# State-space part: the exchange of real and imaginary halves as SBUF to SBUF transfers instead of fp32 products on TensorE

## The chip, the cores and the metric

The kernel runs on one core of a Trainium2 chip. The metric is the device time of one execution, in microseconds (us).

## What the reference computes

One layer of a hybrid model for 1024 new tokens of one stream (`TP`) and 64 further tokens of a running one (`TS`), 1088 in all (`T`): an RMS norm, one large input projection, three branches (a pooling mixer, a state-space mixer, an attention with forget gates), three sigmoid gates per channel that weigh the branches, an output projection, and a gated feed-forward layer with a short convolution. The change is in the state-space mixer:

```python
lam_bar = jnp.exp(lam * dt)                        # complex, per state
bu = jnp.einsum('gpc,blgc->blgp', b_bar, ug)       # 32 groups, 64 complex states, 16 channels each
_, states = lax.associative_scan(combine, (a, bu), axis=1)   # s[t] = lam_bar * s[t-1] + bu[t]
y = jnp.einsum('gcp,blgp->blgc', c_mat, states).real.reshape(bn, L, W_MIX)
```

## The kernel before

There are two stages, and the state-space mixer stands at the start of the second (`mix_engines`). Each engine has its own list of instructions, executed in order, and engines meet at semaphores. `Steps` counts a semaphore through named steps, so `pe_did.at("v1")` means "TensorE has done step v of tile 1".

The state-space mixer works on four tiles (`t` = 0 to 3) of 8 groups (`NB`) each. Time is cut into chunks of 16 tokens (`C`), 68 of them (`NCH`). The 64 complex states lie on the 128 partitions, real parts on partitions 0 to 63 and imaginary parts on 64 to 127. For each tile:

- TensorE transposes the input matrices (step `et`, L2009), makes the kernel of the chunk (step `k`, L2015) and the inputs of the chunks (step `v`, L2024). ScalarE copies the last from PSUM to `vv` (L2129), 8 groups by 70 columns (`E70`), so 560 fp32 per partition.
- SyncE's list (`toeplitz`, L1889) spreads the chunk kernel in 16 SBUF to SBUF transfers over `tm1` and `tm0`, 8 KB for the smallest and 128 KB for the largest. It does so as soon as step `k` has been copied out.
- The recurrence over chunks has a complex factor, whose angle is taken out first so that VectorE's scan (L2254) is real: `vv` is multiplied by the cosine table (`rc`, L2245) and its copy with exchanged halves by the sine table (`rs`, L2249), and the two are subtracted. After the scan the result `ww` is turned back in the same way (L2256, L2260) and gives `sc` (L2265, L2266), the states ahead of each chunk.
- The copy with exchanged halves is made on TensorE: a product with a 128 by 128 permutation `swap` in fp32, two products of 280 columns each, for `vv` (step `swap_v`, L2030) and for `ww` (step `swap_w`, L2035). The results are read from PSUM.
- TensorE makes the output of the chunks (step `y`, L2042 to L2044) from the input, `tm1`, `tm0` and `sc`, and turns it back (step `back`, L2056).

So that TensorE has work while the others do this, 39 pieces of the gate projection stand between these steps (`gate_pieces`, 24 matmuls each through the helper line L154, or `three_pass`). `SLOTS` says how many follow each step: between `v` and `y` there are three pieces in tiles 0 and 3 and four in tiles 1 and 2. GpSimd splits the gate weights into a high and a low part for these pieces (`split_tile`, L951 to L955), and SyncE's list loads them (`load_gate`): blocks 15 and 16 after the `toeplitz` of tile 0, 19 and 20 after that of tile 1, 23 after that of tile 2, none after that of tile 3. Each such load waits until GpSimd has split the block that held the buffer. VectorE scales each piece (L2183) and ScalarE finishes and stores it.

Of the kernel before, what the change touches and what calls it, by code (L numbers as in the profile page):

```python
# [14 lines left out]
ALU, ACT, AX = mybir.AluOpType, mybir.ActivationFunctionType, mybir.AxisListType  # L15

P = 128
# [18 lines left out]
G32, SC, SS = 32, 16, 64  # L36
NB = 8
E70 = NP_CH + 1 + NS_CH + 1
# [6 lines left out]
class Steps:  # L45
# [15 lines left out]
    def mark(self, name):  # L61
        assert self.names[self.n % len(self.names)] == name, (self.names[self.n % len(self.names)], name)
        self.n += 1
        return self.sem, 1
# [1681 lines left out]
SEVEN = ("et", "k", "v", "swap_v", "swap_w", "y", "back")  # L1746
# [25 lines left out]
def mix_engines(nc, m, io, sems):  # L1772

    ps, sem = m.bank, lambda n: sems(f"mix_{n}")
    gp, r4 = ps[:, 0:4], ps[:, 4:8]
    CS, KP0 = C * SC, 96
    GATE0, NG = GATES_ATT, 3 * (3 * KD - GATES_ATT)
    flat = lambda t: t[:].rearrange("p g e -> p (g e)")
    with ExitStack() as outer:
        y = outer.enter_context(nc.sbuf_tensor("y", [P, MW, T], F32))  # L1780
        with ExitStack() as inner:
            sb = lambda n, s, d=F32: inner.enter_context(nc.sbuf_tensor(n, s, d))
            et, swap = sb("et", [P, 2 * NB, P + 8]), sb("swap", [P, P])
            assert nc.sbuf_base == m.early_at
            sb("early", [P, EARLY // 4])
            m.tab.append(sb("tab1", [P, NB, NTAB]))
            rows = sb("ssm_rows", [P, NB * CS])
            u2 = sb("u2", [P, 2, 2 * NB, NCH])
            cl = sb("cl", [P, NB, C + 1, SC])
            tm1, tm0 = sb("toeplitz1", [P, NB, CS]), sb("toeplitz0", [P, NB, CS // 2])  # L1790
            vv, x1, x2, d0 = (sb(n, [P, NB, E70]) for n in ("vv", "x1", "x2", "d0"))
            sc, sf = sb("sc", [P, NB, NCH]), sb("sf", [P, G32, 2])
            gout = sb("gate_out3", [P, T])
        with ExitStack() as inner:
            sb = lambda n, s, d=F32: inner.enter_context(nc.sbuf_tensor(n, s, d))
            merged, prod, gate = sb("merged", [P, KD * T]), sb("prod", [P, T]), sb("gate", [P, 2, T])
            sig = sb("sig", [P, 2, T])
            yh, yl = sb("y_hi", [P, MW, T], F32R), sb("y_lo", [P, MW, T], F32R)
    ww = x2
# [7 lines left out]
    tiles = range(MW)  # L1807
# [7 lines left out]
    b2_ld, even_mm, prod_done, sum_done, hi, lo = (sem(n) for n in (  # L1815
        "b2_ld", "even_mm", "prod_done", "sum_done", "hi", "lo"))
    ws, gws = m.merge_ws, m.gate_ws
    pe_did = Steps(sem("pe_did"), [f"{n}{t}" for t in tiles for n in SEVEN])
    act_did = Steps(sem("act_did"), [f"{n}{t}" for t in tiles for n in (
        ("et", "kp", "s0_", "vv") + (tuple(f"gelu_hi{k}_" for k in range(3)) if t == 3 else ()) + ("yc",))] +  # L1820
        ["gelu_hi3_3"] + [f"sig{o}" for o in tiles] + [f"r_hi{o}" for o in tiles])
# [8 lines left out]
    halves = lambda t: t[:].rearrange("p g e -> p (g e)").rearrange("p (b n) -> p b n", b=2)  # L1830
# [17 lines left out]
    def sync(sp):  # L1848
        def load_tab(t):
            if t >= 2:  # L1850
                sp.wait_ge(*pe_did.at(f"y{t - 2}"))
            sp.dma_start(tab[t % 2][:], m.tab_d[:, t * NB:(t + 1) * NB]).then_inc(tab_ld[t % 2], 16)
# [28 lines left out]
        def toeplitz(t):  # L1881
# [4 lines left out]
            for r in range(C):  # L1886
                rows = slice(r % 8 * SC, (r % 8 + 1) * SC)
                dst, c0, cn = (tm1, (C - 1 - r) * SC, CS) if r >= 8 else (tm0, (7 - r) * SC, CS // 2)
                sp.dma_start(dst[rows, :, c0:cn], kp[:, :, 0:cn - c0]).then_inc(tm_ld, 16)  # L1889

        load_tab(1)
        load_frames(0)
        for t in tiles:
            load_u(t)
        for t, (early, late) in enumerate((((14,), (15, 16)), ((17, 18), (19, 20)), ((21, 22), (23,)), ((), ()))):
            for n in early:
                load_gate(n)
            if t == 3:
                load_glu(0)
                load_glu(1)  # L1900
            toeplitz(t)
            for n in late:
                load_gate(n)
            if t < 3:
                load_frames(t + 1)
            if t < 2:
                load_tab(t + 2)
# [68 lines left out]
    def tensor(pe):  # L1976
# [21 lines left out]
            return mm  # L1998

        gate_pieces(0, "start")  # L2000
        pe.wait_ge(consts, 2)
        for t in tiles:
            j = t % 2
            if t:
                pe.wait_ge(*dve_did.at(f"yt{t - 1}"))
            pe.wait_ge(*pool_did.at(f"w{t}"))
            for n in range(2 * NB):
                g, h = n // 2, n % 2
                mm = pe.transpose(r4[:, n // 4, n % 4 * P:(n % 4 + 1) * P], w[:, g, 8 * h:8 * h + 8], m.ident[:])  # L2009
            mm.then_inc(*pe_did.mark(f"et{t}"))  # L2010
            gate_pieces(t, "et")
            pe.wait_ge(*act_did.at(f"et{t}"))
            pe.wait_ge(*dve_did.at(f"et{t}"))
            for g in range(NB):
                mm = pe.matmul(r4[0:SC, g // 2, g % 2 * CS:(g % 2 + 1) * CS], tab[j][:, g, B1:B1 + SC],  # L2015
                               cl[:, g, 0:C], start=True, stop=True)
            mm.then_inc(*pe_did.mark(f"k{t}"))
            gate_pieces(t, "k")
            pe.wait_ge(*act_did.at(f"kp{t}"))
            pe.wait_ge(*dve_did.at(f"kp{t}"))  # L2020
            pe.wait_ge(u2_ld[j], 256 * (t // 2 + 1))
            for g in range(NB):
                for h in range(2):
                    mm = pe.matmul(r4[:, g // 4, g % 4 * NCH:(g % 4 + 1) * NCH], et[:, 2 * g + h, 0:P],  # L2024
                                   u2[:, j, 2 * g + h], start=h == 0, stop=h == 1)
            mm.then_inc(*pe_did.mark(f"v{t}"))
            gate_pieces(t, "v")
            pe.wait_ge(*act_did.at(f"vv{t}"))
            for h in range(2):
                mm = pe.matmul(r4[:, h, 0:NSW], swap[:], halves(vv)[:, h], start=True, stop=True)  # L2030
            mm.then_inc(*pe_did.mark(f"swap_v{t}"))
            gate_pieces(t, "swap_v")
            pe.wait_ge(*dve_did.at(f"ww{t}"))
            for h in range(2):
                mm = pe.matmul(r4[:, h, 0:NSW], swap[:], halves(ww)[:, h], start=True, stop=True)  # L2035
            mm.then_inc(*pe_did.mark(f"swap_w{t}"))
            gate_pieces(t, "swap_w")
            pe.wait_ge(*dve_did.at(f"sc{t}"))
            pe.wait_ge(tm_ld, 256 * (t + 1))
            for g in range(NB):  # L2040
                out = r4[0:NCH, g // 2, g % 2 * CS:(g % 2 + 1) * CS]
                pe.matmul(out, u2[:, j, 2 * g + 1], tm1[:, g], start=True, stop=False)  # L2042
                pe.matmul(out[:, CS // 2:CS], u2[:, j, 2 * g], tm0[:, g], start=False, stop=False)
                mm = pe.matmul(out, sc[:, g], cl[:, g, 1:C + 1], start=False, stop=True)  # L2044
            mm.then_inc(*pe_did.mark(f"y{t}"))
            gate_pieces(t, "y")
            if t == MW - 1:
                pe.wait_ge(ws.w_split, 3)
                pe.wait_ge(gate_raw, NG)
                for k in range(3):  # L2050
                    pe.wait_ge(*dve_did.at(f"y_lo{k}_3"))
                    part(0, 0, operand["glu"], [k])
            pe.wait_ge(*act_did.at(f"yc{t}"))
            pe.wait_ge(*dve_did.at(f"yc{t}"))
            for n in range(C):
                mm = pe.transpose(r4[:, n // 4, n % 4 * NCH:(n % 4 + 1) * NCH], yc[:, n], m.ident[0:NCH, 0:NCH])  # L2056
            mm.then_inc(*pe_did.mark(f"back{t}"))
            gate_pieces(t, "back")
# [31 lines left out]
    def scalar(act):  # L2090
# [20 lines left out]
        for t in tiles:  # L2111
# [20 lines left out]
            gate_pieces(t, "swap_v")  # L2132
            gate_pieces(t, "swap_w")
            if t == MW - 1:
                act.wait_ge(*pe_did.at(f"swap_w{t}"))
                act.wait_ge(piece_mm, NG)
                for k in range(3):
                    gelu_high(k)
# [38 lines left out]
    def vector(dve):  # L2177
# [19 lines left out]
        dve.wait_ge(m.o_st[2], 32 + 32 * HEADS)  # L2197
        for g in range(3):
            dve.wait_ge(m.g_st[g], 16 * GATES_ATT)
        for a in range(2):  # L2200
            dve.tensor_copy(swap[:, a * SS:(a + 1) * SS], m.ident[:, (1 - a) * SS:(2 - a) * SS])
        dve.memset(tm1[:], 0.0)
        dve.memset(tm0[:], 0.0)
        dve.memset(vv[:, :, 0:1], 0.0)
# [4 lines left out]
        for t in tiles:  # L2209
# [30 lines left out]
            gate_pieces(t, "k")  # L2240

            rc, rs = tab[j][:, :, RC:RC + E70], tab[j][:, :, RS:RS + E70]
            sw = lambda b: r4[:, b, 0:NSW].rearrange("p (g e) -> p g e", e=E70)
            dve.wait_ge(*act_did.at(f"vv{t}"))
            dve.tensor_tensor(x1[:], vv[:], rc, ALU.mult).then_inc(*mark("x1"))  # L2245
            gate_pieces(t, "v")
            dve.wait_ge(*pe_did.at(f"swap_v{t}"))
            for b in range(2):
                ins = dve.tensor_tensor(x2[:, 4 * b:4 * b + 4], sw(b), rs[:, 4 * b:4 * b + 4], ALU.mult)  # L2249
            ins.then_inc(*mark("x2"))  # L2250
            dve.wait_ge(*at("x2"))
            dve.tensor_tensor(x1[:], x1[:], x2[:], ALU.subtract).then_inc(*mark("d1"))
            dve.wait_ge(*at("d1"))
# [1 line left out]
            dve.wait_ge(*at("ww"))  # L2255
            dve.tensor_tensor(x1[:], ww[:], rc, ALU.mult).then_inc(*mark("x3"))  # L2256
            gate_pieces(t, "swap_v")
            dve.wait_ge(*pe_did.at(f"swap_w{t}"))
            for b in range(2):
                ins = dve.tensor_tensor(vv[:, 4 * b:4 * b + 4], sw(b), rs[:, 4 * b:4 * b + 4], ALU.mult)  # L2260
            ins.then_inc(*mark("x4"))
            dve.wait_ge(*at("x4"))
            dve.tensor_tensor(sf[:, t * NB:(t + 1) * NB], x1[:, :, NP_CH:E70:NS_CH + 1],
                              vv[:, :, NP_CH:E70:NS_CH + 1], ALU.add).then_inc(*mark("sf"))
# [749 lines left out]
```

## Time and profile before

| | |
|---|---|
| median of 3 runs | 1903.46 us (1899.62 to 1903.72) |
| the profiled execution | 1899.79 us, of it the span of the profile 1898.0 us |
| TensorE busy | 98% of the span |
| VectorE, GpSimd, ScalarE busy | 63%, 43%, 23% |
| granted TensorE clock, mean | 0.993 of full speed |
| SyncE's DMA queue | 31.6% of 16 engines' span |

Engines are PE (TensorE), PEld (its weight loads, which overlap), DVE (VectorE), ACT (ScalarE), POOL (GpSimd) and SP (SyncE). An engine's name with a q means its instruction queue, where DMAs are issued. L154 is line 154 of the kernel. Idle time is put down to the engine or DMA that released the waiting instruction last. Matmuls overlap, so that a row's duration is longer than the distance to the next row. The four tiles of the state-space mixer lie between about 594 and 825 us of the span.

### The profile page before, as it was taken

Reading aid. Unit: us, or ns where it says so; the run is one execution under the profiler, and the core shown is the slowest. Engines: PE = TensorE matmul, PEld = TensorE weight load, DVE = VectorE, ACT = ScalarE, POOL = GpSimd, SP = SyncE. Lnnn points to the kernel's source line nnn. Section 1 sums busy time; section 2 is a strip of 40 time slices with the busy share of each in tenths; the row PEclk is TensorE's granted clock in tenths of the full one; section 3 lists DMA queues with packets and bytes.
Section 4 is the critical chain, followed back from the end, with each engine's and each line's share of the span. In section 5 each row is a group of like instructions: output and inputs, shape, how many; then the busy total and the mean of one; then the engine's idle time right before and its main releaser. Section 6 shows DMA issues by size and latency. Waiting matters only on the chain. (4 is left out here: it accounts for less than half of the span.)

```text
span 1898.0 us, 28823 instructions
## 1 busy us (share of the span) xinstructions
PE 1854.0 (98%) x11323; PEld 1804.3 (95%) x11323; DVE 1193.7 (63%) x1820; ACT 433.0 (23%) x812; POOL 807.0 (43%) x461
## 2 busy tenths in 40 slices
PE   7999999999999999999999999999999999999997
PEld 6989999999989898999999999999999999999997
DVE  6788653888875545542673667557557557557556
ACT  4210123556641111140010231111111111111113
POOL 4434444333356446322232454625625625625520
PEclk8999999999999999999999999999999999999999
DMA  8634829676625454356441111101101101101102
GB/s 271 186 126 129 264 106 261 159 189 172 173 83 144 116 118 100 68 219 229 137 163 45 35 54 56 56 22 55 55 22 55 55 22 55 52 26 55 45 23 97
DMA packets 221950, 203.97 MB, mean 107 GB/s; under 512 B 58306, under 2 KB 200622, under 8 KB 221155
## 3 DMA queue, kind: packets, MB, share of 16 engines
q1 hardware_dynamic: 205650, 170.46, 31.6%
q10 hardware_dynamic: 16208, 32.25, 4.8%
q8 instruction: 62, 1.02, 0.2%
q14 instruction: 30, 0.24, 0.0%
HBM read 138.44 MB, written 59.77 MB: 104 GB/s over the span
## 5 line engine op out<-in xcount | busy, mean ns | idle before, releaser
L154 PE MATMUL bank<-act_hi,w_hi 128*128 128x364 f32 (+1 forms) x2544 | 849.1, 334 | 8.5 <-DVE act_lo L1483 3.7
L154 PE MATMUL bank<-act_lo,w_hi 128*128 128x364 f32 (+1 forms) x2544 | 839.1, 330 | 0.0
L154 PE MATMUL bank<-act_hi,w_lo 128*128 128x364 f32 (+1 forms) x2544 | 838.6, 330 | 0.0
L154 PEld LDWEIGHTS bank<-act_hi,w_hi 128*128 128x128 f32 x2544 | 480.5, 189 | 15.2 <-issue 9.2
L154 PEld LDWEIGHTS bank<-act_lo,w_hi 128*128 128x128 f32 x2544 | 480.3, 189 | 0.8
L154 PEld LDWEIGHTS bank<-act_hi,w_lo 128*128 128x128 f32 x2544 | 480.0, 189 | 0.0
L2769 DVE SCALAR_TENSOR_TENSOR conv<-up_raw,cw,conv 128x1090 f32<-128x1090 f32 x86 | 179.9, 2092 | 63.8 <-ACT up_raw L2655 33.5
L2452 POOL CAST w_hi<-w_raw 128x1024 fp32r<-128x1024 f32 x44 | 47.5, 1079 | 356.9 <-PE bank L154 351.8
L154 PE MATMUL bank<-ffn_hi,down_hi 128*128 128x364 f32 (+1 forms) x528 | 174.0, 330 | 0.7 <-DVE up_raw L2803 0.5
L154 PE MATMUL bank<-ffn_lo,down_hi 128*128 128x364 f32 (+1 forms) x528 | 173.0, 328 | 0.0
L154 PE MATMUL bank<-ffn_hi,down_lo 128*128 128x364 f32 (+1 forms) x528 | 172.7, 327 | 0.0
L2792 DVE TENSOR_TENSOR xt<-bank,xt 128x364 f32<-128x364 f32 (+1 forms) x240 | 113.4, 527 | 76.9 <-PE bank L154 76.3
L2761 DVE TENSOR_TENSOR up_raw<-bank,n_inv 128x364 f32<-128x364 f32 x129 | 58.0, 505 | 139.8 <-PE bank L154 139.6
L953 POOL CAST w_hi<-w_raw 128x1024 fp32r<-128x1024 f32 x36 | 46.0, 1278 | 201.2 <-PE bank L154 200.3
L2443 POOL TENSOR_TENSOR w_raw<-w_raw,vec 128x1024 f32<-128x1024 f32 x44 | 116.0, 2635 | 17.1 <-PE bank L154 13.0
L2454 POOL TENSOR_TENSOR w_lo<-w_raw,w_hi 128x1024 fp32r<-128x1024 f32 x44 | 109.4, 2487 | 3.5
L154 PEld LDWEIGHTS bank<-ffn_hi,down_hi 128*128 128x128 f32 x528 | 99.1, 188 | 1.4 <-DVE up_raw L2803 0.8
L154 PEld LDWEIGHTS bank<-ffn_lo,down_hi 128*128 128x128 f32 x528 | 99.4, 188 | 0.0
L154 PEld LDWEIGHTS bank<-ffn_hi,down_lo 128*128 128x128 f32 x528 | 99.0, 188 | 0.0
L2660 ACT ACTIVATE last<-up_raw 128x2 f32 (+1 forms) x86 | 13.4, 204 | 360.3 <-DVE up_raw L2762 355.5
L955 POOL TENSOR_TENSOR w_lo<-w_raw,w_hi 128x1024 fp32r<-128x1024 f32 x36 | 92.9, 2580 | 2.9
L1225 POOL CAST w_hi<-w_raw 128x1024 fp32r<-128x1024 f32 x20 | 24.7, 1236 | 147.8 <-PE bank L154 147.7
(302 smaller groups left out, 2462.6 us busy)
## 6 DMA issues: line engine op xcount, KB each, us to landing
w_raw<-in_w_up SPq DMA_DIRECT2D x44, 512.0 KB, 3.8
w_raw<-in_w_in SPq DMA_DIRECT2D x42, 512.0 KB, 4.8
gate<-gate_scratch ACTq DMA_DIRECT2D x24, 544.0 KB, 3.8
w_raw<-in_w_down SPq DMA_DIRECT2D x22, 512.0 KB, 3.3
gate_scratch<-gate_out ACTq DMA_DIRECT2D x48, 182.0 KB, 2.7
w_raw<-in_w_branch SPq DMA_DIRECT2D x12, 512.0 KB, 3.9
kh<-kh_scratch SPq DMA_DIRECT2D x16, 336.0 KB, 7.4
kl<-kl_scratch SPq DMA_DIRECT2D x16, 336.0 KB, 8.2
```

The costliest lines, as they stand in the source:

```text
L154: mm = pe.matmul(out, w(k), x(k)[:, c0:c0 + cn], start=first and k == ks[0] and n == 0, stop=last and k == ks[-1] and n == 2)
L953: pool.tensor_copy(m.wh[:, a], m.raw[:, a]).then_inc(s.w_hi, 1)
L955: pool.tensor_tensor(m.wl[:, a], m.raw[:, a], m.wh[:, a].bitcast(F32), ALU.subtract).then_inc(s.w_split, 1)
L1225: pool.tensor_copy(m.wh[:, a], m.raw[:, a]).then_inc(w_hi, 1)
L2443: pool.tensor_tensor(m.raw[:, a], m.raw[:, a], by_channel(m.vec[:, 8:16]), ALU.mult).then_inc(*pool_did.mark(f"sc_{blk}"))
L2452: pool.tensor_copy(hi[:, a], m.raw[:, a]).then_inc(*pool_did.mark(f"hi_{blk}"))
L2454: pool.tensor_tensor(lo[:, a], m.raw[:, a], hi[:, a].bitcast(F32), ALU.subtract).then_inc(*pool_did.mark(f"lo_{blk}"))
L2660: ins = act.activation(by_tile(last[:, n], 2)[:, bass.ds(f, 1)], up[:, a, c0:c0 + 2].unsqueeze(1), ACT.Copy)
L2761: dve.tensor_tensor(up[:, a, HP + c0:HP + c0 + n], acc[a][:, g, 0:n], inv[:, c0:c0 + n], ALU.mult)
L2769: dve.scalar_tensor_tensor(out=cv[:, a], in0=up[:, a, t:UP - 2 + t], scalar=m.cw01[:, bass.ds(f + 44 * t, 1)], in1=cv[:, a], op0=ALU.mult, ...
L2792: ins = dve.tensor_tensor(m.xt[:, d, c0:c0 + cn], acc[d % 2][:, g, 0:cn], m.xt[:, d, c0:c0 + cn], ALU.add)
```

## The change

The permutation `swap` and the 16 fp32 products are taken out, with their steps in `pe_did`. SyncE's list gets a function `exchange`, which copies partitions 0 to 63 of `vv` or `ww` to partitions 64 to 127 of a buffer and the other half the other way, in two transfers of 64 rows of 2,240 bytes. The two buffers (`other`) lie in the memory of `et`, which is free between step `v` and the next tile. In SyncE's list the first exchange stands behind `toeplitz(t)` and waits for `vv`; then come one gate load, a wait for `ww`, the second exchange, and the remaining loads. VectorE waits for the landing, and its products with the sine table read SBUF instead of PSUM, in one instruction of 560 columns instead of two of 280. The slots of the gate pieces stay as they were.

```diff
-            et, swap = sb("et", [P, 2 * NB, P + 8]), sb("swap", [P, P])
+            et, _ = sb("et", [P, 2 * NB, P + 8]), sb("gap", [P, P])
...
+    swapped = sem("swapped")
+    other = [flat(et)[:, n * NB * E70:(n + 1) * NB * E70] for n in range(2)]
...
+        def exchange(n, src):
+            for a in range(2):
+                sp.dma_start(other[n][SS * a:SS * (a + 1)], flat(src)[SS * (1 - a):SS * (2 - a)]).then_inc(swapped, 16)
...
             toeplitz(t)
-            for n in late:
+            sp.wait_ge(*pe_did.at(f"v{t}"))
+            sp.wait_ge(*act_did.at(f"vv{t}"))
+            exchange(0, vv)
+            for n in late[:1]:
+                load_gate(n)
+            sp.wait_ge(*dve_did.at(f"ww{t}"))
+            exchange(1, ww)
+            for n in late[1:]:
                 load_gate(n)
...
         gate_pieces(0, "start")
-        pe.wait_ge(consts, 2)
...
             gate_pieces(t, "v")
-            pe.wait_ge(*act_did.at(f"vv{t}"))
-            for h in range(2):
-                mm = pe.matmul(r4[:, h, 0:NSW], swap[:], halves(vv)[:, h], start=True, stop=True)
-            mm.then_inc(*pe_did.mark(f"swap_v{t}"))
             gate_pieces(t, "swap_v")
-            pe.wait_ge(*dve_did.at(f"ww{t}"))
-            for h in range(2):
-                mm = pe.matmul(r4[:, h, 0:NSW], swap[:], halves(ww)[:, h], start=True, stop=True)
-            mm.then_inc(*pe_did.mark(f"swap_w{t}"))
             gate_pieces(t, "swap_w")
             pe.wait_ge(*dve_did.at(f"sc{t}"))
...
             if t == MW - 1:
-                act.wait_ge(*pe_did.at(f"swap_w{t}"))
                 act.wait_ge(piece_mm, NG)
...
-        for a in range(2):
-            dve.tensor_copy(swap[:, a * SS:(a + 1) * SS], m.ident[:, (1 - a) * SS:(2 - a) * SS])
...
-            dve.wait_ge(*pe_did.at(f"swap_v{t}"))
-            for b in range(2):
-                ins = dve.tensor_tensor(x2[:, 4 * b:4 * b + 4], sw(b), rs[:, 4 * b:4 * b + 4], ALU.mult)
-            ins.then_inc(*mark("x2"))
+            dve.wait_ge(swapped, 64 * t + 32)
+            dve.tensor_tensor(x2[:], sw(0), rs, ALU.mult).then_inc(*mark("x2"))
...
-            dve.wait_ge(*pe_did.at(f"swap_w{t}"))
-            for b in range(2):
-                ins = dve.tensor_tensor(vv[:, 4 * b:4 * b + 4], sw(b), rs[:, 4 * b:4 * b + 4], ALU.mult)
-            ins.then_inc(*mark("x4"))
+            dve.wait_ge(swapped, 64 * t + 64)
+            dve.tensor_tensor(vv[:], sw(1), rs, ALU.mult).then_inc(*mark("x4"))
```

## Rows read from the trace of the kernel before

**Rows 1.** The page: busy time of each engine, share of the span, instructions.

```profile
PE 1854.0 (98%) x11323; PEld 1804.3 (95%) x11323; DVE 1193.7 (63%) x1820; ACT 433.0 (23%) x812; POOL 807.0 (43%) x461
```

**Rows 2.** Windows over the four tiles: busy time by engine, then clock, DMA.

```profile
595.00:660.00 65.00, 63.22 (x394) 57.02 (x393) 35.18 (x36) 10.12 (x20) 36.60 (x19) 1.00 0.48 116
660.00:785.00 125.00, 125.00 (x770) 113.30 (x769) 66.37 (x71) 19.72 (x40) 66.48 (x31) 1.00 0.42 96
785.00:825.00 40.00, 39.13 (x248) 35.87 (x246) 16.44 (x25) 14.53 (x21) 6.77 (x4) 1.00 0.69 189
```

**Rows 3.** Timeline of PE in tile 0: start, duration, line, operation.

```profile
611.19 0.41 PE L154 MATMUL bank<-act_hi,w_hi 128*128 128x364 f32 x1
...
615.27 1.10 PE L2030 MATMUL bank<-vv,swap 128*128 128x280 f32 x4
...
620.21 1.10 PE L2035 MATMUL bank<-x,swap 128*128 128x280 f32 x4
...
625.19 0.59 PE L2042 MATMUL bank<-toeplitz,u 128*68 128x256 f32 x2
```

**Rows 4.** Timelines of DVE and POOL in tile 0.

```profile
612.36 2.72 DVE L2245 TENSOR_TENSOR x<-vv,tab 128x560 f32<-128x560 f32 x1 [3.92 <-ACT vv L2129]
...
612.09 2.39 POOL L955 TENSOR_TENSOR w_lo<-w_raw,w_hi 128x1024 fp32r<-128x1024 f32 x1
...
624.56 1.90 POOL L951 TENSOR_TENSOR w_raw<-w_raw,gain 128x1024 f32<-128x1024 f32 x1 [10.08 <-DMA w_raw<-in_w_in]
```

**Rows 5.** Timeline of SP's queue: the 16 `toeplitz` issues of each tile.

```profile
604.96 11.83 SPq L1889 DMA_DIRECT2D toeplitz<-ssm_rows  x16
...
615.72 1.08 SPq L1889 DMA_DIRECT2D toeplitz<-ssm_rows  x1
...
663.93 11.81 SPq L1889 DMA_DIRECT2D toeplitz<-ssm_rows  x16
...
725.83 11.40 SPq L1889 DMA_DIRECT2D toeplitz<-ssm_rows  x16
...
785.02 11.66 SPq L1889 DMA_DIRECT2D toeplitz<-ssm_rows  x16
```

**Rows 6.** DMA issues: size, median us from issue to landing.

```profile
toeplitz<-ssm_rows SPq DMA_DIRECT2D x1, 16.0 KB, 1.9
...
toeplitz<-ssm_rows SPq DMA_DIRECT2D x1, 128.0 KB, 5.8
...
gate_scratch<-gate_out ACTq DMA_DIRECT2D x48, 182.0 KB, 2.7
```

**Rows 7.** Timeline of DVE in tile 0, from `x2` to `sc`.

```profile
616.41 0.81 DVE L2249 TENSOR_TENSOR x<-bank,tab 128x280 f32<-128x280 f32 x2 [0.41 <-PE bank L2030]
...
618.03 1.32 DVE L2254 TENSOR_TENSOR_SCAN x<-d,x 128x560 f32<-128x560 f32 x1
...
621.35 0.81 DVE L2260 TENSOR_TENSOR vv<-bank,tab 128x280 f32<-128x280 f32 x2 [0.41 <-PE bank L2035]
...
622.90 0.18 DVE L2266 TENSOR_TENSOR sc<-x,vv 128x32 f32<-128x32 f32 x1
```

**Rows 8.** Timeline of PE: the first matmul of step `y`, tiles 1 to 3.

```profile
687.70 0.59 PE L2042 MATMUL bank<-toeplitz,u 128*68 128x256 f32 x2
...
748.51 0.59 PE L2042 MATMUL bank<-toeplitz,u 128*68 128x256 f32 x2
...
805.16 0.59 PE L2042 MATMUL bank<-toeplitz,u 128*68 128x256 f32 x2
```

**Rows 9.** Windows around two falls of the clock, columns as in rows 2.

```profile
348.00:351.00 3.00, 1.58 (x11) 0.99 (x10) 3.00 (x3) 0.91 (x5) 2.14 (x1) 1.00 0.99 215
351.00:354.50 3.50, 3.50 (x15) 3.50 (x14) 2.40 (x8) 1.87 (x4) 0.46 (x1) 0.51 1.03 300
552.00:556.00 4.00, 1.53 (x10) 0.98 (x8) 4.00 (x3) 0.70 (x3) 3.92 (x3) 0.98 0.00 0
556.00:563.00 7.00, 5.96 (x22) 5.20 (x23) 4.48 (x13) 1.62 (x5) 2.22 (x1) 0.52 0.44 112
```

More of the change, by code:

```diff
@@ L1817, in mix_engines @@
     ws, gws = m.merge_ws, m.gate_ws
-    pe_did = Steps(sem("pe_did"), [f"{n}{t}" for t in tiles for n in SEVEN])
+    pe_did = Steps(sem("pe_did"), [f"{n}{t}" for t in tiles for n in SEVEN if "swap" not in n])
+    swapped = sem("swapped")
+    other = [flat(et)[:, n * NB * E70:(n + 1) * NB * E70] for n in range(2)]
     act_did = Steps(sem("act_did"), [f"{n}{t}" for t in tiles for n in (
@@ L2242, in vector @@
             rc, rs = tab[j][:, :, RC:RC + E70], tab[j][:, :, RS:RS + E70]
-            sw = lambda b: r4[:, b, 0:NSW].rearrange("p (g e) -> p g e", e=E70)
+            sw = lambda n: other[n].rearrange("p (g e) -> p g e", e=E70)
             dve.wait_ge(*act_did.at(f"vv{t}"))
```

## The prediction, made before the changed kernel was run

> **What bounds the kernel now.** I read the page first, for the engine that is never idle. TensorE is busy 98% of the span [rows 1], so work taken off it is time gained and a wait put on it is time lost. The windows over the four tiles of the state-space mixer say the same of this stretch: 227.4 of 230 us busy, and from 660 to 785 us without a gap, at full clock [rows 2]. So the fp32 products with the permutation do cost time now, and what matters is whether TensorE still finds `sc` ready when it comes to step `y`. For that I read the timelines of tile 0 on one clock: TensorE [rows 3], VectorE and GpSimd [rows 4], then SyncE's queue with its landings [rows 5, 6].
>
> **What is removed.** One gate piece takes 615.27 - 611.19 = 4.08 us. From the first permutation product to the second, with one piece between, are 4.94 us, and from the second to step `y`, again with one piece, 4.98 us [rows 3]. The products thus hold TensorE for 0.86 and 0.90 us, 1.76 us a tile, 7.0 us in all. This is the whole gain, and it is there only if nothing else makes TensorE wait. The two copies that built `swap`, the removed waits for `consts` and `swap_w`, and the memory change cost and give nothing: behind them in tile 0 TensorE has four pieces of gate work to do (4.08 us each), longer than the copies, and the other two waits were over before they were reached.
>
> **What is added: the exchange stands in a queue.** In tile 0, `vv` is ready at 612.36, when VectorE starts on it [rows 4]. But SyncE's list is then in the middle of the 16 issues of `toeplitz`, from 604.96 to 616.79 (0.74 us each) [rows 5]. Call the end of these issues E; it is 616.79, 675.74, 737.23 and 796.68 in the four tiles. The first exchange cannot be issued before E. Nor can it land soon after it: the smallest `toeplitz` transfer lands 1.9 us after its issue, the last one 5.8 us [rows 6], because the transfers pile up on the DMA engines. The last, issued at 615.72, lands at 621.5, which is E + 4.7.
>
> The exchange's own data are two transfers of 64 x 2,240 bytes, 280 KB. The trace shows no transfer of this shape. From below it costs nothing (it moves beside the tail of `toeplitz`). From above it goes at the rate of `toeplitz`, itself SBUF to SBUF: 1088 KB between 606.9 (first issue and 1.9) and 621.5, 75 KB per us, so 3.8 us. The nearest row by size and by spread over partitions is the gate store, 182 KB in 2.7 us, 0.8 us above the 1.9 [rows 6]; for 280 KB that gives 1.2 us, which I take. `toeplitz` is slower in that it moves from 16 partitions only. The exchange lands at E + 5.9.
>
> Then VectorE: from the start of `x2` to the end of the scan are 616.41 to 619.35, 2.9 us [rows 7]: E + 8.8. The second exchange has an empty queue: 0.6 us until the second of its transfers is issued (between 0.4 and 0.74), then 1.9 + 1.2, so 3.7 us: E + 12.5. From `x4` to the last part of `sc` are 621.35 to 623.08, 1.7 us [rows 7], and 0.2 for the signals: E + 14.4.
>
> **What is moved: products from PSUM to SBUF.** `x2` and `x4` now read both operands from SBUF. The row of that kind is `x1`: 2.72 us in tile 0, beside a GpSimd operation from 612.09 to 614.48, against 0.81 for the pair that reads PSUM [rows 4, 7]. So each of the eight can cost 0 or 1.9 us more. GpSimd splits a gate block in part of these stretches (in tile 0 from 624.56 on, more than once in the later ones); I take a third, 0.6 us for each tile at one of its two. That makes X = 15.0, where X is the distance from E to step `y`.
>
> The Trainium skill ("SBUF — State Buffer", section "SBUF: two separate sides") states that a VectorE instruction with two SBUF inputs and a GpSimd one that reads SBUF lock each other out for the whole instruction. By that rule the change puts eight instructions under the lock that had been free of it, and the sum would have 15.2 us there where all were caught, and 2.4 by my choice. The row of `x1` agrees.
>
> **The sum.** Before, step `y` starts at 625.19, 687.70, 748.51 and 805.16 [rows 3, 8], which is E + 8.4, 12.0, 11.3 and 8.5, 40.1 us together. The start moves by 4 X - 40.1 = 60.0 - 40.1 = +19.9 us; the 1.76 a tile are in it already, since TensorE is through with its pieces at E + 6.6, 10.2, 9.5 and 6.7 and idles until E + 15.0: 8.4, 4.8, 5.5 and 8.3 us. Nothing later gives this back, because TensorE has no gaps to fill [rows 2].
>
> On top comes the clock. Twice in the trace it fell to half (1.2 of 2.4 GHz) after TensorE had been idle for a part only: busy 1.58 of 3 us, then 3.5 us at 0.51; busy 1.53 of 4 us, then about 7 us at 0.52 [rows 9]. In such a stretch half the time is lost, 1.75 or 3.5 us. The four new idles are longer than either. I take the smaller, 4 x 1.75 = 7.0 us; the bounds are 0 and 14.
>
> The Trainium skill ("TensorE: Matmul & The Clock Gate", section "HAM oscillation — how this bites in real kernels") tells of the same loss in a kernel whose matmuls wait for DMAs between groups. By that rule it comes in all four tiles, without it the sum is +19.9; the falls in the rows agree.
>
> The remaining edits are free. The second of the late gate loads goes out later than now, by about the distance of the two exchanges, but GpSimd's next split of it waits for gate pieces that come later still. Queued behind the wait for `ww` are also the loads of `u2` and tables; they are wanted one tile later. The wait of the gate load that stands ahead of the second exchange (block 23 in tile 2) is over before the scan is: it hangs on the split that follows the piece behind step `v`. If it came 1 us behind the scan instead, tile 2 would lose that 1 us.
>
> So +19.9 + 7.0 = +26.9 us: span 1898.0 to 1924.9, profiled execution 1899.8 to 1926.7. The median of before stands 3.7 us above its profiled execution, so I reckon from the middle, 1901.6, and say 1928 us.
>
> **Rivals.**
> - No loss of clock: the idles pass without a fall. +19.9, 1921 us. Against it: two falls after shorter idles [rows 9].
> - Locked products: all eight are held 1.9 us by GpSimd, 15.2 instead of 2.4: 1941 us. Slow data, 3.8 us for each exchange, comes to the same: X 5.2 larger, +20.8, 1949 us. For it: `x1` in [rows 4]; against it: GpSimd is idle for half of this stretch [rows 2].
> - The exchange isn't held by the tail of `toeplitz`: it lands 0.6 + 3.1 after E, X = 12.8 with the lock, +11.1, 1913 us, and with the clock 1920; without the lock and at 1.9 us per landing X would be 9.8 and the change even.
> - Faster: the transfers are hidden. It is decided by SyncE's issues: if they didn't hold the exchange, it would start at 612.4 in tile 0, and `sc` would be there at 612.4 + 3.7 + 2.9 + 3.7 + 1.9 = 624.6, 1.2 us after TensorE's pieces end at 623.4. Tiles 0 and 3 then gain 0.6 each, tiles 1 and 2 with their fourth piece 1.76 each: -4.7, 1897 us, and -7.0, 1895 us, if they land quicker. The point is X = 10.0; my X would have to be a third smaller. The order of SyncE's list speaks against it.
>
> **How the numbers follow.** My own case 0.50; no loss of clock 0.18; locked or slow 0.14; not held by the tail 0.10; hidden 0.04; about even by a mixture 0.04. The likeliest is 1928 with its own range of 1920 to 1937 (the clock 0 to 14, X a us either way). Low bound of all unknown costs: X = 4.7 + 0 + 2.9 + 0.4 + 1.9 + 1.7 = 11.6, +6.3, 1908; high bound: X = 19.5 with 14 for the clock, +52, 1953. The range that leaves 2 in 10 outside is 1911 to 1944. A measurement of this kernel tells about 0.2% (3.8 us) from no change: slower 0.92, same 0.04, faster 0.04.
>
> **What would show it.** In the profile after: no rows of L2030 and L2035; TensorE idle ahead of step `y` in all four tiles, released by VectorE's `sc`, 8 us in tiles 0 and 3 and 5 us in 1 and 2; exchange issues right behind the last `toeplitz` issue; a first landing about 5 us after issue and a second one about 3; granted clock below 1 after each idle. The prediction is wrong if the exchange lands within 2 us, or the idles in tiles 1 and 2 are missing.

## The result

The changed kernel takes 1937.36 us (median of 4 runs, 1936.76 to 1937.62) against 1901.54 us for the kernel before (median of 4, 1899.07 to 1903.72). The ratio is 1.019, with a 95% interval of 1.0176 to 1.0205: slower by 35.8 us. The forecast was 1928 us, +26.9 us, in a range of 1911 to 1944. One execution in experiment 4 (4788 us) and one in experiment 6 (2612 us) stand far outside the others of their kernels and are left out of the medians.

The span of the profiled execution grew from 1898.0 to 1935.8 us, by 37.8 us. The waits of PE between 590 and 870 us name the place. Columns are line, what it waited for, us in total, times, longest.

```profile
PE bank L2046 <- DVE sc L2263: 32.3, 4, 10.2
```

L2046 is the first matmul of step `y` (L2042 before), and `bank` is the PSUM that it writes. There was no such wait in the kernel before. The timeline of PE has its four places, to be set beside [rows 3, 8]; the bracket is the idle time.

```profile
634.67 1.12 PE L2046 MATMUL bank<-toeplitz,u 128*68 128x256 f32 x2 [9.68 <-DVE sc L2263]
...
703.09 0.70 PE L2046 MATMUL bank<-toeplitz,u 128*68 128x256 f32 x1 [5.03 <-DVE sc L2263]
...
771.89 0.69 PE L2046 MATMUL bank<-toeplitz,u 128*68 128x256 f32 x1 [7.33 <-DVE sc L2263]
...
839.36 0.69 PE L2046 MATMUL bank<-toeplitz,u 128*68 128x256 f32 x1 [10.23 <-DVE sc L2263]
```

The timeline of SP's queue, which answers to [rows 5], has the two exchanges as `et<-vv` and `et<-x`:

```profile
606.55 11.85 SPq L1891 DMA_DIRECT2D toeplitz<-ssm_rows  x16
618.51 4.07 SPq L1895 DMA_DIRECT2D et<-vv  x2
622.63 0.59 SPq L1870 DMA_DIRECT2D w_raw<-in_w_in  x1
627.92 1.10 SPq L1895 DMA_DIRECT2D et<-x  x2
...
676.06 11.73 SPq L1891 DMA_DIRECT2D toeplitz<-ssm_rows  x16
...
743.74 13.59 SPq L1891 DMA_DIRECT2D toeplitz<-ssm_rows  x16
...
810.72 12.35 SPq L1891 DMA_DIRECT2D toeplitz<-ssm_rows  x16
```

And the timeline of DVE in tile 0, which answers to [rows 7], with one POOL row from the same stretch. In the text `x1` and `x2` are the products of `vv` and of its copy with the two tables and `d1` is their difference; `x3` and `x4` are the same products of `ww` behind the scan; `sf`, made just ahead of `sc`, holds the last states.

```profile
625.02 0.74 DVE L2249 TENSOR_TENSOR x<-et,tab 128x560 f32<-128x560 f32 x1 [7.41 <-DMA et<-vv]
...
626.57 1.32 DVE L2253 TENSOR_TENSOR_SCAN x<-d,x 128x560 f32<-128x560 f32 x1
627.93 2.25 DVE L2255 TENSOR_TENSOR x<-x,tab 128x560 f32<-128x560 f32 x1
...
630.83 0.83 DVE L2258 TENSOR_TENSOR vv<-et,tab 128x560 f32<-128x560 f32 x1 [0.21 <-DMA et<-x]
631.70 2.21 DVE L2260 TENSOR_TENSOR sf<-x,vv 128x16 f32<-128x16 f32 x1
...
634.44 0.18 DVE L2263 TENSOR_TENSOR sc<-x,vv 128x32 f32<-128x32 f32 x1
...
631.15 2.71 POOL L955 TENSOR_TENSOR w_lo<-w_raw,w_hi 128x1024 fp32r<-128x1024 f32 x1
```

With E the end of the `toeplitz` issues (606.55 + 11.85 = 618.40), the steps of the forecast read: first exchange used at E + 6.6, end of the scan at E + 9.5, second exchange used at E + 12.4, `sc` done at E + 16.2, step `y` at E + 16.3. The product behind the second exchange is short again (0.83), but `sf`, 16 columns wide, takes 2.21 us where its median in the kernel before was 0.19: it stands beside the GpSimd instruction that runs from 631.15 to 633.86.

The windows show the clock (columns as in [rows 2]):

```profile
625.00:634.60 9.60, 0.00 (x0) 0.00 (x0) 9.23 (x10) 0.50 (x1) 6.39 (x3) 0.75 0.69 171
634.70:640.00 5.30, 5.30 (x15) 3.40 (x16) 0.36 (x1) 0.51 (x1) 0.00 (x0) 0.50 0.37 90
640.00:645.00 5.00, 5.00 (x30) 3.63 (x29) 0.00 (x0) 0.00 (x0) 0.00 (x0) 1.00 0.00 0
```

TensorE idles for 9.6 us, then works for 5.3 us at half clock (1.2 GHz) and does 15 matmuls in them, against 30 in the next 5.0 us at 2.4 GHz. The other tiles have 5.0, 4.5 and 5.3 us of work at 0.50.

**Where the 37.8 us are.** E + 16.3, 15.3, 14.6 and 16.3 for the four `y` make 62.5, against 40.1 before: 22.4 us. The `toeplitz` issues, two of which are longer than in [rows 5] (13.59 for 11.40, 12.35 for 11.66), add 2.8. Another 1.6 us are there already at the first transposes of tile 0 (595.83 for 594.23). Only the two copies that built `swap` were changed ahead of that point, and this start lies between 592.3 and 596.4 in the profiled executions of all the kernels here, changed or not, so I put the 1.6 us down to the execution. Of the 11.0 us that remain, 0.8 come behind the last step `back`, outside the mixer. The other 10.2 come behind the four starts of `y`, where the clock is low: 20.1 us of work at half speed lose 10 us.

### The profile page after: what moved, and what is told of

It is laid out like the page before. It is cut to its first block and busy times, and to the rows that moved or that the text cites. A ratio compares the mean times of both kernels' runs of the same rounds, so it can differ in the third digit from the quotient of the medians.

```text
span 1935.8 us, 28767 instructions
## 1 busy us (share of the span) xinstructions
PE 1854.5 (96%) x11291; PEld 1800.3 (93%) x11291; DVE 1199.7 (62%) x1810; ACT 433.1 (22%) x812; POOL 808.2 (42%) x461
```

## The experiments

Two theories stood at the start. A: the first exchange is held by what stands ahead of it, the issues of `toeplitz` on SyncE and their transfers on the DMA engines. B: each exchange costs its own landing, whatever stands ahead of it.

**1. Only the first exchange as a transfer, the second on TensorE again**

```diff
-            sp.wait_ge(*dve_did.at(f"ww{t}"))
-            exchange(1, ww)
...
             gate_pieces(t, "swap_v")
+            pe.wait_ge(*dve_did.at(f"ww{t}"))
+            for h in range(2):
+                mm = pe.matmul(r4[:, h, 0:NSW], swap[:], halves(ww)[:, h], start=True, stop=True)
+            mm.then_inc(*pe_did.mark(f"swap_w{t}"))
             gate_pieces(t, "swap_w")
```

> Only the exchange of vv is a transfer; the one of ww is the fp32 product on TensorE again. Theory A (the first exchange stands behind the 16 toeplitz issues and their tail): ww is ready about E + 9.5 as in the changed kernel, TensorE has to wait for it ahead of its product (about 7 us in each tile, clock falls too), and the pieces behind the product come on top, so step y is later than before by 6 us in tiles 0 and 3 and by 7 us in 1 and 2: +26 us and about +9 for the clock, 1933 to 1940 us, as bad as the whole change. Theory B (each of the eight exchanges costs its own landing, alike for both): half of the change's +36, about 1920 us.

1934.56 us, ratio 1.0182 (1.0165 to 1.0199). The waits of PE:

```profile
PE bank L2042 <- DVE x L2259: 30.0, 4, 8.4
```

Here L2042 is the product with `ww`, and TensorE waits ahead of it for the scan. The first exchange alone costs as much as both, as theory A had it. It is so dear because TensorE's list is executed in order: here the wait stands ahead of the product with `ww`, and the gate pieces behind that product come on top.

**2. Only the second exchange as a transfer, the first on TensorE again**

```diff
-            sp.wait_ge(*pe_did.at(f"v{t}"))
-            sp.wait_ge(*act_did.at(f"vv{t}"))
-            exchange(0, vv)
...
             gate_pieces(t, "v")
+            pe.wait_ge(*act_did.at(f"vv{t}"))
+            for h in range(2):
+                mm = pe.matmul(r4[:, h, 0:NSW], swap[:], halves(vv)[:, h], start=True, stop=True)
+            mm.then_inc(*pe_did.mark(f"swap_v{t}"))
             gate_pieces(t, "swap_v")
```

> Only the exchange of ww is a transfer; the one of vv is the fp32 product on TensorE again. Theory A: the scan ends 2.6 us after the last toeplitz issue as in the kernel before, so the transfer goes out right behind the tail and lands about E + 6.6, sc about E + 8.5: level with TensorE in tiles 0 and 3, hidden in 1 and 2, where the removed product gives 0.9 us each. Sum -2 to +4 us: 1900 to 1905 us. Theory B: half of the change's +36, about 1920 us.

1917.26 us, ratio 1.0101 (1.0074 to 1.0127). That is the number of theory B, and my sum for A missed it. But the tiles are not alike, as B wants them: TensorE's idles ahead of `y` are 8.2, 1.1, 4.3 and 1.6 us. The timelines of SP's queue and of DVE, tile 0 and then tile 3:

```profile
616.24 1.33 SPq L1870 DMA_DIRECT2D w_raw<-in_w_in  x1
618.77 1.96 SPq L1895 DMA_DIRECT2D et<-x  x2
...
626.61 1.50 DVE L2265 TENSOR_TENSOR vv<-et,tab 128x560 f32<-128x560 f32 x1 [6.28 <-DMA et<-x]
...
815.36 1.18 SPq L1895 DMA_DIRECT2D et<-x  x2
...
819.29 0.74 DVE L2265 TENSOR_TENSOR vv<-et,tab 128x560 f32<-128x560 f32 x1 [2.36 <-DMA et<-x]
```

In tile 0 a gate load of 512 KB is in the queue ahead of the exchange, and `x4` starts 7.8 us after the issue; in tile 3 no load stands there, and it is 3.9 us. Tiles 1 and 2 have a load ahead as well, and 7.3 and 5.7 us. I had left that load in its place without pricing it. This was still an inference; experiment 5 tests it. The queue is not all of it: instructions between the landing and `y` are stretched beside GpSimd's split here too, by 3.6 us in tile 0 (the `x4` above takes 1.50 us instead of 0.74, `sf` 0.90 instead of 0.19, the last part of `sc` 2.33 instead of 0.19), by 2.4 in tile 2 and by 0.8 in tile 3. Nearly half of the 15.1 us of idle is of this kind.

**3. Both exchanges on ScalarE's queue**

```diff
+            act.wait_ge(*act_did.at(f"vv{t}"))
+            exchange(0, vv)
             gate_pieces(t, "v")
+            act.wait_ge(*dve_did.at(f"ww{t}"))
+            exchange(1, ww)
```

(`exchange` issues from ScalarE here, and SyncE's list is as in the kernel before.)

> Both exchanges are transfers, but issued on ScalarE's queue instead of SyncE's, the first as soon as vv is written. Theory A: the wait for SyncE's issues and for the tail of its queue is gone, the first exchange lands before VectorE wants it, the second about 3 us after the scan; TensorE's idle ahead of step y falls from 8 us a tile to 0 to 1.5 us, the clock doesn't fall, and the change gives 0 to 5 us: 1896 to 1902 us. Rival (the DMA engines themselves are full of toeplitz, whichever queue the exchange stands in): it lands as late as before, at E + 6, and the time stays at 1930 us or more.

1922.16 us, ratio 1.0109 (1.0092 to 1.0126). Neither came true. Of the 35.8 us 15 are gone, and TensorE's waits for `sc` fall from 32.3 to 21.2 us. The timelines of ACT's and SP's queues and of DVE, tile 0:

```profile
614.28 1.95 ACTq L2107 DMA_DIRECT2D et<-vv  x2
...
621.22 0.74 DVE L2248 TENSOR_TENSOR x<-et,tab 128x560 f32<-128x560 f32 x1 [3.29 <-DMA et<-vv]
...
619.59 3.41 SPq L1870 DMA_DIRECT2D w_raw<-in_w_in  x2
...
624.13 1.12 ACTq L2107 DMA_DIRECT2D et<-x  x2
...
630.55 2.48 DVE L2257 TENSOR_TENSOR vv<-et,tab 128x560 f32<-128x560 f32 x1 [5.23 <-DMA et<-x]
```

The first exchange no longer waits for SyncE, but takes 6.9 us beside the `toeplitz` transfers. The second takes 6.4 us beside two gate loads and the loads of `u2`, where it took 2.9 us in the changed kernel, which sends one gate load 5 us ahead of it and the rest after it. So the queue is only a part; what moves at the same time counts as well.

**4. The toeplitz transfers left out** (14 of 16 in each tile)

```diff
-            for r in range(C):
+            for r in range(2):
...
-            pe.wait_ge(tm_ld, 256 * (t + 1))
+            pe.wait_ge(tm_ld, 32 * (t + 1))
```

(and the other counts of `tm_ld` in the same way)

> The changed kernel with 14 of the 16 toeplitz transfers of each tile left out (the two smallest stay, so that the later waits have something to count); the part of the output that comes from them is wrong. The kernel before never waited for them, so its time is still the one to compare with. Theory A (the first exchange is held by the 16 issues and their tail on the DMA engines): the first exchange goes out as soon as vv is ready and lands about 3 us later, sc comes about 1 us after TensorE's pieces in tiles 0 and 3 and ahead of them in 1 and 2, the clock stays up, and the change is a gain of 3 to 7 us: 1895 to 1900 us. Theory B (the exchange lands late by itself, whatever stands ahead): at most a third of the loss goes, 1925 us or more.

1903.39 us, ratio 1.0017 (1.0005 to 1.0029), which is 2.8 us above the kernel before that was timed beside it (1900.56). The waits of PE, and the timelines of SP's queue and DVE in tile 0:

```profile
PE bank L2046 <- DVE sc L2263: 6.4, 2, 3.6
...
613.18 1.16 SPq L1895 DMA_DIRECT2D et<-vv  x2
...
616.71 0.73 DVE L2249 TENSOR_TENSOR x<-et,tab 128x560 f32<-128x560 f32 x1
...
619.60 1.10 SPq L1895 DMA_DIRECT2D et<-x  x2
...
622.52 1.38 DVE L2258 TENSOR_TENSOR vv<-et,tab 128x560 f32<-128x560 f32 x1 [1.73 <-DMA et<-x]
```

The first exchange is there before VectorE asks for it (no idle in the row), the second 2.9 us after its issue. 33.0 of the 35.8 us go with the 14 transfers: theory A is shown and B has fallen. This experiment takes away the issues, the queue and the traffic of `toeplitz` together, so it does not say which of them counts. The time misses my range by 3 us, because 6.4 us of idle stay in tiles 0 and 2, and behind the one of tile 2 the granted clock is 0.50 for 5.0 us. In both tiles GpSimd's split stretches instructions of the chain: in tile 0 `sf` takes 2.21 us, in tile 2 the scan 3.40.

**5. Both on ScalarE's queue, and SyncE's loads behind the second exchange**

```diff
             toeplitz(t)
-            sp.wait_ge(*pe_did.at(f"v{t}"))
-            sp.wait_ge(*act_did.at(f"vv{t}"))
-            exchange(0, vv)
-            for n in late[:1]:
-                load_gate(n)
-            sp.wait_ge(*dve_did.at(f"ww{t}"))
-            exchange(1, ww)
-            for n in late[1:]:
+            sp.wait_ge(swapped, 64 * t + 64)
+            for n in late:
                 load_gate(n)
```

(SyncE's list against that of the changed kernel; ScalarE's is that of experiment 3.)

> As the kernel with the exchanges on ScalarE's queue, and SyncE's late gate loads and the loads of u2 wait until the second exchange has landed. That run had idles of 8.7, 0.9, 6.5 and 5.2 us ahead of y, with second exchanges of 5 us and more that ran beside the loads. Theory (the DMA engines are shared, so what is ahead of the exchange on any queue delays it): the second exchange lands in 3 us, the idles become about 3.5, 0, 2 and 5, and the time 1906 to 1911 us. Rival (the second exchange is slow on this queue by itself): 1920 us or more.

1906.41 us, ratio 1.0027 (1.0016 to 1.0039). The waits of PE and the second exchange in tile 0:

```profile
PE bank L2036 <- DVE sc L2261: 9.9, 4, 4.8
...
627.11 0.74 DVE L2256 TENSOR_TENSOR vv<-et,tab 128x560 f32<-128x560 f32 x1 [1.79 <-DMA et<-x]
```

The scan ends at 624.10 there, so the second exchange takes 3.0 us instead of 6.4. The edit differs from experiment 3 only in when SyncE's loads go, so the 3.4 us are what moves beside the exchange. The idle ahead of `y` in tile 0 falls by more, from 8.7 to 3.2 us, because GpSimd's split has moved away with the load: `x4` takes 0.74 us here and 2.48 there. The two together are also what theory A missed in experiment 2. In tile 3, where no gate load comes late, 4.8 of 5.2 us of idle stay.

**6. TensorE kept busy while it waits**

```diff
             gate_pieces(t, "swap_w")
+            pe.wait_ge(*act_did.at(f"vv{t}"))
+            for n in range((32, 12, 24, 34)[t]):
+                pe.matmul(r4[:, n % 4, 0:P], m.ident[:], m.ident[:], start=True, stop=True)
             pe.wait_ge(*dve_did.at(f"sc{t}"))
```

> The changed kernel, with 32, 12, 24 and 34 fp32 products of identity by identity (128 columns, about 0.22 us each) on TensorE ahead of its wait for sc, into PSUM that step y overwrites; they fill the idle but for 1 to 3 us. Theory: the wait stays as long, but the clock doesn't fall (or for much less), so 8 to 10 us come back: 1927 to 1930 us, granted clock 1.0 behind each wait. Rival (the clock in the records costs nothing): 1937 us as the changed kernel.

1927.96 us, ratio 1.0141 (1.0121 to 1.0161): 9.4 us less than the changed kernel. The windows over the same stretches of tile 0:

```profile
625.00:634.60 9.60, 7.12 (x64) 6.92 (x62) 9.24 (x10) 0.50 (x1) 6.16 (x3) 1.00 0.68 170
634.70:640.00 5.30, 5.30 (x30) 3.86 (x31) 0.34 (x1) 0.51 (x1) 0.00 (x0) 1.00 0.39 92
```

Step `y` starts at 634.64 as before, and 30 matmuls follow in 5.3 us instead of 15. The products compute nothing that is used, so what comes back is the price of the clock. In the traces the stretch from the first transposes of tile 0 to the last step `back` is shorter by 6.8 us; the rest of the 9.4 lies outside it, and I can't put it down to these four waits. The clock still fell behind tiles 1 and 3 (0.58 from 700.5 to 704.6 us, 0.68 from 833.6 to 839.0), which loses another 3.4 us: 6.8 and 3.4 are the 10.2 us of the sum above.

**7. GpSimd's splits moved away from the exchange**

```diff
         for n in (14, 15, 16):
+            if n == 15:
+                pool.wait_ge(*dve_did.at("sc0"))
             gate_split(n)
```

(and in the same way block 18 behind `sc1`, 22 behind `sc2`, and the first stage's second block of GLU weights behind `sc3`)

> The changed kernel, with GpSimd's split that falls on the exchange (blocks 15, 18 and 22, and the first one of the next stage) made to wait for sc of the tile, so that no VectorE instruction between the first exchange and sc stands beside one of GpSimd. In the trace of the changed kernel these instructions are stretched by 2.0, 1.1, 2.0 and 2.7 us in the four tiles. Theory: step y comes that much earlier, 7 to 8 us in all: 1929 to 1931 us. Rival (the stretch is not GpSimd's doing, or what is delayed on GpSimd is missed later): 1936 us or more.

1927.2 us, ratio 1.0139 (1.0122 to 1.0155): 10.2 us less, some 2 us more than I had expected. The end of the chain in tile 0, on DVE:

```profile
629.64 0.74 DVE L2266 TENSOR_TENSOR vv<-et,tab 128x560 f32<-128x560 f32 x1 [1.72 <-DMA et<-x]
630.42 0.19 DVE L2268 TENSOR_TENSOR sf<-x,vv 128x16 f32<-128x16 f32 x1
```

`sf` is at 0.19 again, TensorE's waits for `sc` fall from 32.3 to 24.0 us, and TensorE has no new wait for what GpSimd delivers. Inside the mixer the traces differ by 8.7 us, a little more than the waits.

**8. More gate pieces ahead of `y`**

```diff
-SLOTS = ([("start", 5)] + [(n, 2 if n in ("y", "back") else 1) for n in SEVEN],
+SLOTS = ([("start", 5)] + [(n, {"swap_w": 3, "y": 0, "back": 2}.get(n, 1)) for n in SEVEN],
...
+         [(n, {"swap_w": 4, "y": 0, "back": 2}.get(n, 1)) for n in SEVEN],
```

> The changed kernel with the two gate pieces behind step y moved ahead of it, in tiles 0, 1 and 2 (five, six and six pieces between v and y, none between y and back). Theory (the wait is only uncovered time, 4.08 us of pieces cover 4.08 us of it): the idle of 9.7, 5.0 and 7.3 us ahead of y falls to 1.5, 0 and 0, that of tile 3 stays at 10, about 1.5 us of new idle come ahead of back in each of the three, and the clock falls in tile 3 only: -16 and -7, about 1914 us. Rival (the pieces themselves then wait for VectorE or GpSimd): 1925 us or more.

1916.07 us, ratio 1.0086 (1.0069 to 1.0103), within 2 us of the expectation, though not in every part. The waits of PE:

```profile
PE bank L2046 <- DVE sc L2263: 14.1, 2, 10.6
PE bank L2060 <- DVE ssm_rows L2271: 4.4, 3, 1.5
```

Tiles 1 and 2 have no wait for `sc` left, and the three waits ahead of `back` appear. Tile 0 keeps 3.5 us of idle instead of 1.5, and the clock is low in tile 0 as well (0.61 from 633.3 to 637.0 us), which I had not expected.

**9. The repaired version and its control.** Experiment 5 with one more piece ahead of `y` in tiles 0 and 1, and one moved from tile 2 to tile 3:

```diff
+SLOTS = ([("start", 5)] + [(n, {"swap_w": 2, "y": 1, "back": 2}.get(n, 1)) for n in SEVEN],
+         [(n, {"swap_w": 3, "y": 1, "back": 2}.get(n, 1)) for n in SEVEN],
+         [(n, {"swap_w": 2, "y": 1, "back": 2}.get(n, 1)) for n in SEVEN],
+         [(n, 2 if n == "swap_w" else 1) for n in SEVEN[:5]])
```

> As the kernel with the exchanges on ScalarE's queue and the late loads behind the second exchange; in addition one gate piece of tiles 0 and 1 moves from behind y to ahead of it, and tile 3 gets one more piece ahead of y, taken from behind y of tile 2 (4, 5, 4 and 4 pieces between v and y). That run's idles of 3.2, 1.6, 0 and 4.8 us should fall to 0, 0, 0 and below 1, and the clock's loss of some 5 us (half speed for 4.6 and 6.0 us of work) with them: -13 us from 1906, 1892 to 1896 us, 5 to 8 us faster than the kernel before, which is the price of the products (7.0 us). Rival (the pieces ahead of y are missed between y and back, or the splits come late): 1900 us or more.

1892.61 us, ratio 0.9961 (0.995 to 0.9973): 8.3 us faster than the kernel before it was timed against (1900.86). The waits of PE and the window over the four tiles:

```profile
PE bank L2037 <- DVE sc L2262: 0.2, 1, 0.2
...
595.00:860.00 265.00, 261.30 (x1622) 241.07 (x1621) 140.59 (x144) 53.68 (x96) 121.92 (x60) 1.00 0.52 142
```

The control is the kernel before with the same slots.

> Control: the kernel before, with the products on TensorE, and the same new slots of the gate pieces as the run beside it. It has no idle ahead of y to fill, so if the gain there comes from the products taken away and not from the slots, this one stays at 1899 to 1903 us. If the slots gain by themselves, it goes below 1898 us.

1902.94 us, ratio 1.001 (1.0001 to 1.0019). The slots alone gain nothing; the gain is that of the products taken off TensorE, once the exchange is covered.

**10. The same slots, the exchanges on SyncE's queue, the first in the midst of `toeplitz`**

```diff
             for r in range(C):
+                if r == 10:
+                    sp.wait_ge(*pe_did.at(f"v{t}"))
+                    sp.wait_ge(*act_did.at(f"vv{t}"))
+                    exchange(0, vv)
```

(all late loads behind the second exchange)

> As the first of these three (new slots, late loads behind the second exchange), but the exchanges stay on SyncE's queue, the first between the tenth and the eleventh toeplitz issue. Theory (what counts is what stands ahead in the ring): the first exchange lands about 4 us after vv, but the second is behind the last six, largest toeplitz transfers and lands about E + 7, so sc comes near E + 9.5, about 1 to 2 us before TensorE has done its extra piece (E + 10.5) in tiles 0 and 3: 1894 to 1900 us. Rival (ScalarE's ring is needed): idles of 3 us and more ahead of y in tiles 0 and 3, 1905 us or more.

1896.44 us, ratio 0.9976 (0.9966 to 0.9986). PE's wait for `sc` is 0.3 us in all. The median is 3.8 us above that of experiment 9, but the mixer itself takes the same time in both. The rows of the transposes and of step `back`, with the start of the first and of the last, for the kernel before, experiment 9 and experiment 10:

```profile
L2009 PE MATMUL bank<-ident,ssm_w x64: 270/272/273, 594.2 to 775.9; 128*128 128x128 f32 x64
L2056 PE MATMUL bank<-ident,ssm_rows x64: 223/226/228, 641.8 to 819.2; 68*128 68x68 f32 x64
...
L2012 PE MATMUL bank<-ident,ssm_w x64: 270/273/273, 592.3 to 764.5; 128*128 128x128 f32 x64
L2051 PE MATMUL bank<-ident,ssm_rows x64: 223/226/228, 638.0 to 810.0; 68*128 68x68 f32 x64
...
L2021 PE MATMUL bank<-ident,ssm_w x64: 270/273/273, 595.2 to 767.3; 128*128 128x128 f32 x64
L2060 PE MATMUL bank<-ident,ssm_rows x64: 223/226/228, 640.8 to 812.9; 68*128 68x68 f32 x64
```

From the first start to the last are 225.0 us before and 217.7 us in both experiments (225.8 in the control). So ScalarE's queue is not needed for the gain inside the mixer; the place in the order is. Why the medians lie 3.8 us apart is open.

## Why the prediction was right, and where it was off

**The gain, 7.0 us.** Right. With all waits covered the mixer is 7.3 us shorter in the traces of experiments 9 and 10. The medians are 8.3 us lower in experiment 9, with an interval of 5.1 to 9.5, and 4.4 in experiment 10.

**The first exchange at E + 5.9.** Right: E + 6.6, 6.6, 4.9 and 6.0, and experiment 4 shows that it is `toeplitz` that holds it. What the step had not in it is that the exchange's own two issues take 4.07, 3.43, 1.89 and 3.57 us in the four tiles, against 1.10 for those of the second. The data are used 2.4 to 3.1 us after these issues end, in each tile. So the sum came out right with another split of its terms, and whether the slow issues themselves delay the chain was not separated from the tail.

**Scan, second exchange, `sc`.** The second exchange was put at 3.7 us and takes 2.9. Which of its terms was too large, the issue, the landing or the 1.2 us for the data, was not separated. From the start of `x2` to the end of the scan are 2.9 us where nothing interferes, as forecast.

**Products under GpSimd: the step that was mis-sized.** I took 0.6 us a tile, for `x2` and `x4` alone, because only these change their operands. In the trace `sf` (+2.0) in tiles 0 and 2, `x2` (+1.1) in tile 1 and `d1` and the scan (+2.7) in tile 3 are stretched, 7.8 us in all for 2.4. In the rows of tiles 1 and 3, `x2` and the scan take 1.83 and 3.35 us, where they take 0.74 and 1.32 undisturbed:

```profile
694.41 1.83 DVE L2249 TENSOR_TENSOR x<-et,tab 128x560 f32<-128x560 f32 x1 [7.76 <-DMA et<-vv]
...
693.25 2.39 POOL L955 TENSOR_TENSOR w_lo<-w_raw,w_hi 128x1024 fp32r<-128x1024 f32 x1
...
831.35 3.35 DVE L2253 TENSOR_TENSOR_SCAN x<-d,x 128x560 f32<-128x560 f32 x1
...
830.80 2.71 POOL L955 TENSOR_TENSOR w_lo<-w_raw,w_hi 128x1024 fp32r<-128x1024 f32 x1
```

`d1`, the scan and `sf` had two SBUF operands before the change as well. They are hit because the chain now runs when GpSimd splits a block: a shifted chain meets new neighbours. Experiment 7 confirms the cause. The 5.4 us too little here and the 3.1 us too much for the second exchange (four times 0.8) cancel in part, and so 22.4 us stand against 19.9: that it came this near is in part luck. The Trainium skill ("SBUF — State Buffer", section "SBUF: two separate sides") states the lock for every VectorE instruction with two SBUF inputs, not for new ones only; the stretched rows agree.

**The clock: 10.2 us for 7.0.** I took 1.75 us a tile, the smaller of two falls in [rows 9]. The new idles of 5 to 10 us are longer than those that came before either fall, and each was followed by 4.5 to 5.3 us of work at half speed, 2.5 us of loss. Experiment 6 gives 6.8 us of it back inside the mixer and leaves 3.4. The larger of the two rows would have been too much, so the value lies between.

**The issues of `toeplitz`, 2.8 us.** Not forecast. I had E fixed at the durations of before. Why the 16 issues of tile 2 take 13.59 us instead of 11.40 was not looked into.

**The rivals.** "No loss of clock" has fallen (experiment 6). "Locked products" was true in a part, on other instructions. The prediction says that locked and slow come to the same; by its own sums they do not (+12.8 and +20.8 us on its 1928), and slow data did not come at all: the second exchange was quicker than assumed. "Not held by the tail" and "hidden" have fallen for this order of the queues, and both become true with another one: experiments 9 and 10 are the hidden case, with its -7, reached by an earlier exchange and by a piece more to cover it. The point of X = 10.0 was not tested by itself, since those two have other slots.

**The free edits.** True for the gate load that goes out later. But a load left ahead of an exchange is not free: the second exchange took up to 3.9 us longer behind it in experiment 2 (7.8 for 3.9).

## What to carry to other kernels

Work taken off the engine that bounds the kernel pays only if what replaces it lands in time, and for a transfer that is decided by everything that stands ahead of it: the issues on its engine's list, the transfers in its queue, and those on other queues that move at the same time. Send the transfer that a chain waits for ahead of the bulk loads, and move enough independent work under its flight. When a chain is shifted in time, check which other engine's work it now meets, also for its unchanged instructions.

## What the runs showed of the hardware

- A transfer pair of 2 x 140 KB from SBUF to SBUF was used 2.9 us after its first issue with nothing ahead of it; 6.4 us on another queue than two loads of 512 KB and the loads of `u2` beside it; 7.8 us behind one such load and the end of `toeplitz` in its own queue.
- Two issues of the same shape took 1.10 us on SyncE with nothing ahead in its queue, and 1.89 to 4.07 us right behind 16 other transfers.
- Each idle of 5 to 10 us on TensorE was followed by 4.5 to 5.3 us of its work at 1.2 GHz. Filling it with unused products brought back 6.8 us over four idles, with 3.4 us still lost to falls behind two of them.
- A VectorE instruction on 16 columns took 2.21 us instead of 0.19 beside a GpSimd instruction.
